# Heads paired across key groups, and the values of four jobs as one feature-major product

## The reference

```python
s_c = einsum("bqgrd,bkgd->bgrqk", qb, k_cmp) * scale     # 31 compressed keys
o_c = einsum("bgrqk,bkgd->bqgrd", masked_softmax(s_c, ...), v_cmp)
o_s = ... masked_softmax(qb . ks) . vs                   # selected keys
o_w = ... masked_softmax(qb . kw) . vw                   # window keys
o = gb[..., 0:1] * o_c + gb[..., 1:2] * o_s + gb[..., 2:3] * o_w
```

## Time and profile before

| what | value |
|---|---|
| time, median of 3 runs | 2247.55 us (2246.56 to 2248.97) |
| span of the profiled execution | 2246.4 us |
| TensorE busy | 2224.9 us (99%) |
| VectorE, ScalarE, POOL busy | 1245.1, 885.6, 280.7 us |
| chain that ended last | PE 93%, DVE 3%, POOL 1%, ACT 1%, issue 1% |
| scores of job 0 start | 134.82 us |
| scores of jobs 8, 16, 24 start | 162.85, 191.18, 223.18 us |
| first product after step 31 | 256.67 us |

### The profile page before, as it was taken

The page is one execution under the profiler, slowest core; times in us unless marked ns, Lnnn a source line. Parts: engine busy times, 40 slices in busy tenths (PEclk is TensorE's granted clock), DMA queues, the critical chain, the costliest instruction groups (busy, mean ns, idle before and its releaser), DMA issues.

```text
span 2246.4 us, 29245 instructions
## 1 busy us (share of the span) xinstructions
PE 2224.9 (99%) x11388; PEld 1821.7 (81%) x11388; DVE 1245.1 (55%) x1836; ACT 885.6 (39%) x1363; POOL 280.7 (12%) x273
## 2 busy tenths in 40 slices
PE   9999999999999999999999999999999999999999
PEld 7877888898888888886778888888887668888887
DVE  6467656445444225999664444333889664544422
ACT  5545454354333225234744333222323753433321
POOL 3000032011000001014331000001003442000000
PEclk9999999999999999999999999999999999999999
DMA  6221033122222231321122222222221112322222
GB/s 223 100 76 57 20 121 126 55 72 99 103 102 93 94 113 69 113 75 57 56 77 81 107 93 93 100 106 105 104 84 57 39 66 85 113 102 104 94 101 86
DMA packets 30484, 203.19 MB, mean 90 GB/s; under 512 B 3504, under 2 KB 4144, under 8 KB 6704
## 3 DMA queue, kind: packets, MB, share of 16 engines
q1 hardware_dynamic: 29088, 197.34, 24.4%
q10 hardware_dynamic: 1296, 4.46, 0.5%
HBM read 199.69 MB, written 2.10 MB: 90 GB/s over the span
## 4 chain that ended last, share of the span: by engine, by line
PE 93%; DVE 3%; POOL 1%; ACT 1%; issue 1%; DMA 0%; ACTq 0%; DVEq 0%; POOLq 0%
PE bank L415 26%; PE bank L417 26%; PE bank L416 26%; PE bank L2110 1%; PE bank L1002 1%; PE bank L2120 1%; PE bank L2133 1%; PE bank L973 1%; PE bank L2028 1%; POOL acc L324 1%; PE bank L990 1%; PE bank L2010 1%; PE bank L1593 1%; PE bank L1570 1%; PE bank L515 1%
## 5 line engine op out<-in xcount | busy, mean ns | idle before, releaser
L415 PE MATMUL bank<-x_hi,w_hi 128*128 128x512 f32 (+1 forms) x2032 | 789.9, 389 | 5.9 <-DVE x_lo L1766 2.3
L417 PE MATMUL bank<-x_hi,w_lo 128*128 128x512 f32 (+1 forms) x2032 | 775.0, 381 | 0.0
L416 PE MATMUL bank<-x_lo,w_hi 128*128 128x512 f32 (+1 forms) x2032 | 774.1, 381 | 0.0
L301 DVE TENSOR_TENSOR w_lo<-w_raw,w_hi 128x2048 fp32r<-128x2048 f32 x167 | 386.2, 2313 | 412.3 <-ACT w_hi L297 412.3
L297 ACT ACTIVATE w_hi<-w_raw 128x2048 fp32r<-128x2048 f32 x167 | 319.7, 1916 | 585.8 <-PE bank L417 583.9
L415 PEld LDWEIGHTS bank<-x_hi,w_hi 128*128 128x128 f32 x2032 | 382.1, 188 | 83.6 <-issue 6.8
L417 PEld LDWEIGHTS bank<-x_hi,w_lo 128*128 128x128 f32 x2032 | 381.9, 188 | 74.9
L416 PEld LDWEIGHTS bank<-x_lo,w_hi 128*128 128x128 f32 x2032 | 382.4, 188 | 72.7 <-issue 2.9
L415 PE MATMUL bank<-f_hi,w_hi 128*128 128x512 f32 (+1 forms) x572 | 213.3, 373 | 0.0
L416 PE MATMUL bank<-f_lo,w_hi 128*128 128x512 f32 (+1 forms) x572 | 213.2, 373 | 0.0
L417 PE MATMUL bank<-f_hi,w_lo 128*128 128x512 f32 (+1 forms) x572 | 213.2, 373 | 0.0
(11 more groups left out here) (355 smaller groups left out, 2637.2 us busy)
## 6 DMA issues: line engine op xcount, KB each, us to landing
w_raw<-w_d SPq DMA_DIRECT2D x184, 1024.0 KB, 4.8
out_d<-h SPq DMA_DIRECT2D x8, 256.0 KB, 6.6
h<-x_d ACTq DMA_DIRECT2D x3, 512.0 KB, 9.2
tab<-rope_d ACTq DMA_DIRECT2D x2, 640.0 KB, 3.9
memT<-mem_d ACTq DMA_DIRECT2D x1, 1024.0 KB, 4.8
w_raw<-w_d SPq DMA_DIRECT2D x2, 256.0 KB, 4.1
h<-x_d ACTq DMA_DIRECT2D x2, 256.0 KB, 5.8
w_raw<-w_d SPq DMA_DIRECT2D x1, 512.0 KB, 6.6
```

Source lines behind the costliest of these rows:

```text
L301: dve.tensor_tensor(w_lo[:, u.slot, :], w_raw[:, u.slot, :], w_hi[:, u.slot, :], ALU.subtract).then_inc(lo_ready, 1)
L415: pe.matmul(dst, wh[:, k, cols], hi[:, kx_, at:at + width], start=start, stop=False)
L416: pe.matmul(dst, wh[:, k, cols], lo[:, kx_, at:at + width], start=False, stop=False)
L417: return pe.matmul(dst, wl[:, k, cols], hi[:, kx_, at:at + width], start=False, stop=stop)
```

## The change

Heads are paired across key groups: (m, m+4), so the key rows of each half of the partitions serve as they are, `kTx` and its copies go, and the columns of the query weights, the gate weights, the gains and the rows of `w_out` are put in the new order on the host. A job is a block, a branch, and a pair `m = j % 4`. TensorE no longer adds the mask. VectorE does, for each head, one operation (`minima`) that reads the scores from the bank, negates them, adds the mask `causal_b`, writes them to `prob` and gives the minimum. ScalarE's `exps` work in place. VectorE computes gate over sum (`weights`), POOL multiplies the probabilities by it (`job_scaled`), TensorE transposes at step `t + 3`, and ScalarE and VectorE copy into `pT`. When four jobs of a branch are there (steps 7, 11, ..., 35) `values(n)` multiplies them at once: 64 value columns are stationary, 512 columns (four pairs by 128 tokens) moving, the two heads in two halves of the output partitions. Both branches accumulate in bank 6; `block_out` adds the bank once a block to `o_all`, which is now feature-major. The compressed branch is done likewise, with its weights applied before the transposes.

The turns of `o_all` at the end go. Its squares are summed over features by POOL (`block_squares_added`) and by column sums on TensorE; the inverse root is spread to rows in bank 6, and VectorE multiplies `o_all` by it. POOL's loop also holds the sums of the convolution's squares and the inverse root, each behind a `job_scaled`.

```diff
+        J_LAG_T, J_LAG_V, C_LAG_T, C_LAG_V = 3, 4, 2, 3
+        J_STEPS = JOBS + J_LAG_V
+        J_VALUES_AT = {js[-1] + J_LAG_V: n for n, js in enumerate(J_GROUPS)}
+
+        def block_end(b_):
+
+            return 8 * b_ + 7 + J_LAG_V
...
-            return j // 8, j % 8 // 2, j % 2, j % 8 // 4
+            return j // 8, j % 4, j % 8 // 4
...
-                pe.wait_ge(j_exp, i + 1)
+                pe.wait_ge(c_w, 4 * i + 4)
...
+                for m in range(4):
+                    for e in range(2):
+                        mm = pe.matmul(bank[HD * e:HD * e + HD, 6, m * P:(m + 1) * P], vblk[:, e, m * HD:(m + 1) * HD],
+                                       pt_c[:, i % 2, e * P:(e + 1) * P], start=True, stop=True)
...
-                if j == 0:
-                    pe.wait_ge(kx_ready, 4)
                 if j < 2:
                     pe.wait_ge(c_sub, QB - 1 + j)
                 else:
-                    pe.wait_ge(j_exp, QB + 2 * (j - 1))
+                    pe.wait_ge(j_max, QB + 2 * (j - 1))
                 for e in range(2):
                     pe.matmul(bank[:, b_ + e, 0:n], qT[HD * e:HD * e + HD, m, i * P:(i + 1) * P],
-                              key_rows(kT, kTx, e, g)[:, br, 0:n], start=True, stop=False)
-                for e in range(2):
-                    mm = pe.matmul(bank[:, b_ + e, i * P:n], ident_b[:, :], mask_b[:, P:2 * P], start=False, stop=True)
-                mm.then_inc(j_s, 1)
+                              kT[HD * e:HD * e + HD, br, 0:n], start=True, stop=True).then_inc(j_s, 1)
...
-                pe.wait_ge(j_exp, QB + 2 * (j + 1))
+                pe.wait_ge(j_scaled, j + 1)
...
-            def values(j):
-                i, m, br, g = job(j)
-                pe.wait_ge(j_pta, QB + j + 1)
-                if wide(j):
-                    pe.wait_ge(j_ptd, turned_by_dve(j))
-                pe.wait_ge(j_o, QB + 2 * j)
-                for e in range(2):
-                    c0 = (j % 2) * 2 * HD + e * HD
-                    for k in range(i + 1):
-                        mm = pe.matmul(bank[:, 6, c0:c0 + HD], probT[:, j % 2, e, k * P:(k + 1) * P],
-                                       vtok[:, k, br * P + g * HD:br * P + (g + 1) * HD], start=(k == 0), stop=(k == i))
+            def values(n):
+                js = J_GROUPS[n]
+                i, m0, br = job(js[0])
+                m1 = m0 + len(js)
+                pe.wait_ge(j_pta, QB + js[-1] + 1)
+                if wide(js[-1]):
+                    pe.wait_ge(j_ptd, turned_by_dve(js[-1]))
+                if br == 0:
+                    pe.wait_ge(j_o, QB + i)
+                for k in range(i + 1):
+                    for e in range(2):
+                        mm = pe.matmul(bank[HD * e:HD * e + HD, 6, m0 * P:m1 * P], vtok[:, k, br * P + e * HD:br * P + (e + 1) * HD],
+                                       pT[:, k, e, m0:m1, :].rearrange("p m t -> p (m t)"),
+                                       start=(br == 0 and k == 0), stop=(br == 1 and k == i))
...
+            TAIL_TILES = {JOBS: (0, 0), JOBS + 1: (0, 1), JOBS + 2: (1, 0), JOBS + 3: (1, 1)}
+            for t in range(-QB, J_STEPS):
                 if t < 0:
                     c_scores(t + QB)
                 elif t < JOBS:
                     scores(t)
+                if 0 <= t + QB - C_LAG_V < QB:
+                    c_values(t + QB - C_LAG_V)
+                if t in J_VALUES_AT:
+                    values(J_VALUES_AT[t])
+                if 0 <= t + QB - C_LAG_T < QB:
+                    c_turn(t + QB - C_LAG_T)
+                if 0 <= t - J_LAG_T < JOBS:
+                    turn(t - J_LAG_T)
                 gated_chunks(GATED_AT.get(t, 0))
                 if t == -QB:
                     compressed_values()
-                if t == JOBS:
-                    pe.wait_ge(mix_lo, 4)
-                    pe.wait_ge(lo_ready, U_OUT + 1)
-                if t >= JOBS:
-                    mixed_products(0, (t - JOBS,), range(4))
-                if -QB <= t - LAG_TURN < 0:
-                    c_turn(t - LAG_TURN + QB)
-                elif 0 <= t - LAG_TURN < JOBS:
-                    turn(t - LAG_TURN)
-                if -QB <= t - LAG_VALUES < 0:
-                    c_values(t - LAG_VALUES + QB)
-                elif t - LAG_VALUES >= 0:
-                    values(t - LAG_VALUES)
+                if t in TAIL_TILES:
+                    j, m = TAIL_TILES[t]
+                    if (j, m) == (0, 0):
+                        pe.wait_ge(mix_lo, 4)
+                        pe.wait_ge(j_max, QB + 2 * JOBS)
+                    if m == 0:
+                        pe.wait_ge(lo_ready, U_OUT + j + 1)
+                    mixed_products(j, (m,), range(4))
...
-            def mixed_turn(m):
-                if m == 0:
-                    pe.wait_ge(ao_n, QB)
-                if m >= 2:
-                    pe.wait_ge(mix_lo, 4 + m - 1)
-                for b_ in range(QB):
-                    mm = pe.transpose(bank[:, 6 + m % 2, b_ * P:(b_ + 1) * P], o_all[:, b_, m * P:(m + 1) * P], ident[:, :])
-                mm.then_inc(ao_t, 1)
-
-            pe.wait_ge(j_exp, QB + 2 * JOBS)
-            pe.wait_ge(lo_ready, U_OUT + 2)
-            mixed_products(1, (0, 1), range(4))
             pe.wait_ge(j_pta, QB + JOBS)
             pe.wait_ge(j_ptd, turned_by_dve(JOBS - 1))
             pe.wait_ge(lo_ready, U_OUT + 3)
             mixed_products(2, (0,), range(4))
-            mixed_turn(0)
-            mixed_turn(1)
+            pe.wait_ge(ao_added, 2 * QB)
+            column_sums(pe, bank[:, 7, 0:QB], acc[:, :]).then_inc(ao_step, 1)
             mixed_products(2, (1,), range(4))
-            mixed_turn(2)
-            mixed_turn(3)
+            pe.wait_ge(ao_step, AO_INV)
+            spread(pe, bank[:, 6, :], small[:, 36:36 + QB]).then_inc(ao_step, 1)
...
+            def c_out(i):
+                act.wait_ge(j_pv, i + 1)
+                act.activation(o_all[:, :, i * P:(i + 1) * P], bank[:, 6, :].rearrange("p (m t) -> p m t", m=4), ACT.Copy).then_inc(j_o, 1)
...
+                for e in range(2):
+                    act.wait_ge(j_max, QB + 2 * j + e + 1)
+                    row = prob[:, j % 4, e, 0:n]
+                    act.activation(row, row, ACT.Exp, bias=jsm(j, 0, e), scale=-1.0, accum_out=jsm(j, 4, e)).then_inc(j_exp, 1)
...
+            def minima(j):
                 n = (j // 8 + 1) * P
-                dve.wait_ge(j_s, QB + j + 1)
+                if j == 0:
+                    dve.wait_ge(unit_done, 11)
+                    dve.wait_ge(pool_made, CAUSAL_MADE)
                 if j >= 4:
-                    dve.wait_ge(j_exp, QB + 2 * (j - 3))
-                dve.tensor_reduce(jsm(j, 0), bank[:, 2 * (j % 2):2 * (j % 2) + 2, 0:n], AX, ALU.max).then_inc(j_max, 1)
-                dve.wait_ge(j_max, QB + j + 1)
-                dve.tensor_scalar(jsm(j, 2), jsm(j, 0), LOW, -1.0, ALU.max, ALU.mult).then_inc(j_neg, 1)
+                    dve.wait_ge(j_t, QB + j - 3)
+                for e in range(2):
+                    dve.wait_ge(j_s, QB + 2 * j + e + 1)
+                    dve.tensor_tensor_reduce(prob[:, j % 4, e, 0:n], bank[:, 2 * (j % 2) + e, 0:n], causal_b[:, T - n:T],
+                                             -1.0, -LOW, ALU.add, ALU.min, jsm(j, 0, e)).then_inc(j_max, 1)
...
                 dve.tensor_tensor(jsm(j, 8), jsm(j, 6), gate[:, i, 6 * m + 1 + br:6 * m + 5 + br:3], ALU.mult).then_inc(j_w, 1)
...
-                dve.wait_ge(j_w, j + 1)
-                dve.wait_ge(j_pv, QB + j + 1)
-                for e in range(2):
-                    o = o_all[:, i, (2 * m + e) * HD:(2 * m + e + 1) * HD]
-                    if br:
-                        dve.wait_ge(j_o, QB + 2 * (j - 1) + e + 1)
-                    else:
-                        dve.wait_ge(j_o, i + 1)
-                    c0 = (j % 2) * 2 * HD + e * HD
-                    dve.scalar_tensor_tensor(out=o, in0=bank[:, 6, c0:c0 + HD], scalar=jsm(j, 8, e), in1=o,
-                                             op0=ALU.mult, op1=ALU.add).then_inc(j_o, 1)
...
+            def block_out(b_):
+                o = o_all[:, :, b_ * P:(b_ + 1) * P]
+                dve.wait_ge(j_pv, QB + J_GROUP_OF[8 * b_ + 7] + 1)
+                dve.tensor_tensor(o, bank[:, 6, :].rearrange("p (m t) -> p m t", m=4), o, ALU.add).then_inc(j_o, 1)
...
-                    maxima(t)
-                if -QB <= t - LAG_TURN < 0:
-                    c_weights(t - LAG_TURN + QB)
-                elif 0 <= t - LAG_TURN < JOBS and wide(t - LAG_TURN):
-                    copy_turned(t - LAG_TURN)
-                if -QB <= t - LAG_VALUES < 0:
-                    c_combine(t - LAG_VALUES + QB)
-                elif t - LAG_VALUES >= 0:
-                    combine(t - LAG_VALUES)
+                    minima(t)
+                if -QB <= t - 1 < 0:
+                    c_weights(t - 1 + QB)
+                elif 0 <= t - 1 < JOBS:
+                    weights(t - 1)
```

(47 more changed lines are left out.)

## The result

The changed kernel takes 2255.45 us (median of 8 runs, 2253.84 to 2256.19), the kernel before 2248.3 us in the same comparison (2246.56 to 2249.52). The ratio is 1.0029, with a 95% interval of 1.0020 to 1.0039: slower by 0.3%. The profiled execution has a span of 2252.4 us against 2246.4, so 6.0 us are to be accounted for; the forecast was +10.0, the difference of the medians is 7.1.

The account below looks back on a forecast made before the run. TensorE, 99% busy, bounds the kernel before; after the change VectorE binds blocks 2 and 3. Terms -1.0 + 3.8 (loop) + 1.2 + 5.2 (tail) + 0.8 (clock) = +10.0, giving 2257.5 us; range 2238 to 2266.

Parts of the forecast that it names:

- blocks 0 and 1: First two blocks of the loop: TensorE sets the pace, 26.0 and 23.0 us, before 28.05 and 28.3.
- TensorE's own in the tail: Tail: two more turns of 0.87 us than before, less 0.5 saved at the end, +1.2 us.
- hole before `k` = 4: Tail, after the spread: TensorE idles for VectorE's products and low parts, 4.8 to 5.7 us, taken as 5.2.
- clock, wherever: TensorE at half clock after holes of 4 to 5 us: +0.8 us net, bounds -1.5 and +5.
- VectorE's own work: Blocks 2 and 3: VectorE's operations over 16 steps sum to 51.8 us, of which minima 22.3.
- lengthened by POOL: Blocks 2 and 3: VectorE operations with both inputs in SBUF collide with POOL's passes, 13.7 us.
- waits, and the lag at the start: Blocks 2 and 3: VectorE waits 3.5 (column sums), 4.5 (spread) and 0.8 us (`block_out`), and starts 2.3 late.
- Rivals C: Whole loop: TensorE stays the bound, its work less 23 us, tail hole 5.2: -18 us, 2230; chance 0.05.
- D: Values: array halves do not overlap, 17.4 us more values, +20 us, 2267; chance 0.08 together with the clock.
- the price of the minimum: VectorE's minima, priced from the second part: 0.50 us for 256 columns, 0.63 for 384, 0.76 for 512.
- rival B: Blocks 2 and 3: half of the VectorE and POOL collisions are hidden, +3 us, 2250.5; chance 0.15.
- rival A: Blocks 2 and 3: VectorE's sum binds but the port shared with POOL does not, -7.5 us, 2240; chance 0.27.

Follow-up runs that it names:

- e7: Changed kernel plus one extra one-column VectorE product behind each of the 32 minima in blocks 2 and 3: 2258.99 us.
- e4: Changed kernel with POOL's scaling cut to 8 columns of each head's probabilities, the rest left out: 2249.45 us.
- e1: Changed kernel with POOL doing the convolution norm's squares and the inverse root ahead of the same step's scaling: 2251.48 us.
- e6: Changed kernel with the convolution's gated products, passes and norm scheduled earlier, column sums at step 20 instead of 23: 2257.55 us.
- e10: Changed kernel with inverse root ahead of scaling, tail reordered, convolution passes one a step from step 15, its low parts spread over three steps: 2243.87 us.
- e3: Changed kernel with VectorE's four products and four low parts in the tail taken in turn: 2253.41 us.
- e5: Changed kernel with VectorE's tail order interleaved and TensorE's column sums and spread moved ahead of mixed products: 2249.25 us.
- e12: As e10, but the last two convolution passes stand together in step 21: 2242.36 us, ratio 0.9975 to the kernel before.

## Why the prediction was right, and where it was not

Forecast 2257.5 us, measured 2255.45; forecast and outcome are both slower by more than 0.2%. The mechanisms were mostly right, several sizes were not: the loop was sized too long and what follows it too short. That the sum came within 4 us of the span's difference is in part luck, since the errors have both signs.

| step | predicted, us | measured in the trace, us |
|---|---|---|
| ahead of the loop | -1.0 | -0.15 (134.67 against 134.82) |
| blocks 0 and 1 | 26.0 + 23.0 | 26.9 + 23.1 |
| blocks 2 and 3 | 76.6 | 69.4 |
| loop, difference | +3.8 | -2.4 |
| TensorE's own in the tail | +1.2 | +1.8 (28.87 - 4.42 - 22.66) |
| hole before `k` = 4 | +5.2 | +4.4 |
| behind the hole | none | +2.2 (10.46 against 8.29) |
| clock, wherever | +0.8 | contained in the above |
| sum | +10.0 | +5.8 of the span's 6.0 |

Blocks 2 and 3 in the prediction's own terms, VectorE's work, collisions and waits:

| term | predicted, us | measured in the trace, us |
|---|---|---|
| VectorE's own work | 51.8 | 46.3 (56.07 busy less 9.8) |
| lengthened by POOL | 13.7 | 9.8 |
| waits, and the lag at the start | 8.8 + 2.3 | 13.4 idle |
| sum | 76.6 | 69.4 |

**TensorE's work.** Right. Values are 0.43 us a pair, heads side by side, and blocks 0 and 1 came within 0.9 us. Rivals C (TensorE the bound) and D (no overlap) fall: TensorE is busy 51.5 of the 69.4 us of blocks 2 and 3, and the pairs are 0.43 us apart.

**The term that was most off: the price of the minimum.** It was read from the second part as busy time over count, 0.50 for 256 columns (each record lasts 539 ns, but overlaps with the next), and extended to 0.63 and 0.76. The extension was right: here too 128 more columns cost 0.13 to 0.14 us. The base was not. From start to start two minima of 512 columns are 0.61 us apart (223.24, 223.85 above), of 384 columns 0.48 (203.91, 204.39), and of 256 columns 0.34 (163.40, 163.74), where the second part's, in the trace before, are 0.47 apart:

```profile
1053.53 0.53 DVE L2415 CUSTOM_DVE_ANT_0 lprob<-bank,mask_b,neg_sink 128x256 f32<-128x256 f32 x1
...
1054.00 0.54 DVE L2415 CUSTOM_DVE_ANT_0 lprob<-bank,mask_b,neg_sink 128x256 f32<-128x256 f32 x1
```

So the second part's operation is itself some 0.12 us dearer at the same width. It takes its factor and its bound from columns with one value per partition (`query_factor`, `neg_sink`), the new one takes them as constants; whether that is the reason no run separates. Sixteen minima of each width cost 17.4 us and not 22.3: 4.9 too much, of which reading from start to start (0.47 instead of 0.50) would have removed only 1. e7 shows that such an error passes into the time in large part or in full.

**VectorE against POOL.** The mechanism is right and shown by e4; the size was off: 13.7 us forecast for blocks 2 and 3, 9.8 us measured there (6.6 by the scaling, which e4 takes away; the rest stays in e4, where POOL still does its sums of squares). Of the 9.1 us that the scaling costs VectorE in the whole loop at most 5.4 reached its end. As to what is hidden this lies close to rival B (half of it), though not in the time. On its own terms rival A (the port doesn't bind) fails: of the two lines that it was to be told by, L1373 (L1370 before) has 1734 ns where A needed 750; the other, L807 (L793 before), met nothing and kept its 1218, but its sibling L811 rose to 1763. The rule of the Trainium skill ("SBUF — State Buffer", Who interferes with whom), that whoever comes first holds the pair for its whole instruction, agrees with L1371, which starts at 200.82 us, 0.25 behind a scaling of 1.47, and takes 1.50 where it took 0.48 before. It gives the length of a collision and says nothing on whether it is hidden.

**Waits.** The root's was right in kind and somewhat small in size: VectorE waited 5.9 us for the scores of job 27 against 4.5 forecast, TensorE 3.2 ahead of the spread, and 3.9 us came back when the root went first. Of the 5.9 a part is half clock: the scores behind the spread, from 229.24, took 2.08 us where the first ones of block 3 took 1.13. Around the column sums VectorE waited 2.5 + 0.9 us against 3.5 forecast, but that the size fits is luck: TensorE waits only 0.4 us for the squares there, and e1 moves them ahead without a gain. What VectorE waits for is 2.80 us of values and the turn behind them, which the estimate had left out and which cover the squares; where no values stand ahead (e6) or the last pass comes a step later (e10) the wait for the squares is 3.1. The wait for `block_out` was 1.9 against 0.8. TensorE's waits for copies, 9.9 us in seven pieces, were in the sum only as VectorE's total, not by their name.

**Tail.** The hole was right (4.4 against 5.2) and so was its cause: e3 halves it and e5 takes it away. What followed it was not forecast: the products behind the hole ran at a mean clock of 0.78, and the low parts met POOL's sums; 2.3 us, returned by e5.

**Clock.** +0.8 with bounds of -1.5 and +5 was too small. In the changed kernel the clock was 0.94 and 0.87 in blocks 2 and 3 where it was 1.00 and 0.95 before, and identical loops differ by 5.8 us with it, more than most terms of the sum.

**Where the gain went.** TensorE's busy time fell by 14.3 us, though more of it ran at half clock. In blocks 2 and 3 this turned into waiting: for VectorE's copies, lengthened by collisions with POOL, for the root, and on VectorE's side for scores and values; they are 3.9 us longer than before. The end lost 8.4 us, more than the 6.4 that blocks 0 and 1 had won. It did not have to: with the root ahead of the scaling and the tail reordered the same change is level with before or a little faster (0.9983 to 1.0001), and with the convolution spaced as well (e12) it gains 0.25%.

## What to carry to other kernels

Taking work off the busiest engine pays only where it is alone at the limit: put the next engine's time beside it stretch by stretch, and ask what the freed time ends in. Check whether a price taken from a similar operation elsewhere has the same operands: here its growth with width was right and its level 0.12 us off, 32 times. When work moves to a third engine, look at what stands behind it in that engine's queue: a short root ahead of a long pass instead of behind it was worth 4 us. Where a chain of norm and scaling hid under other products, keep one of them to run behind its last step: that gave 6 us.

## What the runs showed of the hardware that was not expected

- Two of VectorE's minimum operations in a row overlap: 0.68 us long, 0.61 apart (512 columns); 0.55 long, 0.48 apart (384); 0.42 long, 0.34 apart (256). The second part's form, with a factor and a bound per partition, is 0.54 long and 0.47 apart for 256.
- Executions with the same instructions in the loop lasted 119.4, 121.7 and 125.2 us, at a mean granted clock of 0.94, 0.92 and 0.89, with VectorE's busy time equal to 0.1 us. The longest is of the slowest of eleven executions.
- Raising the granted clock from 0.93 to 0.97 with products that nobody reads gave no time back that could be measured.
- Collisions with the scaling cost VectorE 9.1 us of busy time; without them, and with shorter waits for the scaling, the loop was 5.4 us shorter.
